# Three rounded passes for key, value and receptance in an RWKV layer, with its token differences and modulation columns reordered

## What is computed

```
    xx = h_shift - h
    xr, xw, xk, xv, xa, xg = [h + xx * mix[j] for j in range(6)]
    r = xr @ wr
    k = xk @ wk
    v = xv @ wv
    ...
        wlog = (w0[d] + jnp.tanh(xw @ w1[d]) @ w2[d]).astype(jnp.float32)
        a = jax.nn.sigmoid((a0[d] + (xa @ a1[d]) @ a2[d]).astype(jnp.float32))
```

## Time and profile before

| | |
|---|---|
| Median of 3 executions | 3708.02 us (3697.62 to 3708.9) |
| The profiled execution | 3712.69 us, its span 3710.8 us |
| Busy: TensorE, VectorE, ScalarE, GpSimd | 3444.4, 1473.4, 1101.6, 315.3 us |
| Granted TensorE clock, mean of the span | 0.973 |
| Chain that ended last, by engine | PE 76%, DVE 9%, DMA 8%, ACT 3%, POOL 2% |
| The RWKV projections lie between | 948 and 1276 us of the span |

### The profile page before, as it was taken

One profiled execution on the slowest core, in us unless ns is written; L12 is line 12 of the kernel. 1 busy time (PEld: TensorE's weight loads), 2 busy tenths in 40 slices (PEclk: granted clock), 3 DMA queues, 4 the chain that ended last, 5 costly groups with the idle time before them and its releaser, 6 DMA issues.

```text
span 3710.8 us, 64299 instructions
## 1 busy us (share of the span) xinstructions
PE 3444.4 (93%) x28700; PEld 2265.9 (61%) x28700; DVE 1473.4 (40%) x2588; ACT 1101.6 (30%) x2075; POOL 315.3 (8%) x260
## 2 busy tenths in 40 slices
PE   6999999999799999999779887899999999999998
PEld 4555344335357588888434332266888876878886
DVE  2232001014542267777531000157753435674343
ACT  4121111113442255554210000144532323543131
POOL 0000000000100234444100000001000001000000
PEclk8989999999799999999989999999999999999999
DMA  9236988985434344431527999930242212133320
GB/s 352 81 158 272 376 333 330 380 341 223 153 118 157 94 97 86 85 72 43 183 113 323 421 413 421 421 115 18 74 148 91 91 51 76 41 116 111 91 91 23
DMA packets 340518, 666.56 MB, mean 180 GB/s; under 512 B 156601, under 2 KB 250297, under 8 KB 284945
## 3 DMA queue, kind: packets, MB, share of 16 engines
q1 hardware_dynamic: 330128, 633.14, 47.5%
q10 hardware_dynamic: 6912, 18.88, 1.3%
q0 software_dynamic: 3200, 10.42, 0.8%
HBM read 630.92 MB, written 31.46 MB: 178 GB/s over the span
## 4 chain that ended last, share of the span: by engine, by line
PE 76%; DVE 9%; DMA 8%; ACT 3%; POOL 2%; issue 1%; SPq 1%; DVEq 0%; ACTq 0%; POOLq 0%
PE ps L1072 14%; PE ps L1077 5%; PE ps L714 4%; DMA ring<-in_moe_wu 4%; PE ps L3202 3%; PE ps L3201 3%; PE ps L3200 3%; PE ps L3218 3%; PE ps L3219 3%; PE ps L3217 3%; PE ps L630 3%; PE ps L631 2%; PE ps L632 2%; PE ps L1507 2%; POOL ring L1896 2%; PE ps L1532 2%
## 5 line engine op out<-in xcount | busy, mean ns | idle before, releaser
L1072 PE MATMUL ps<-ring,H 128*64 128x512 f32 x2016 | 483.8, 602 | 43.4 <-DMA ring<-in_moe_wu 32.9
L1183 DVE TENSOR_TENSOR scr<-ps,scr 128x512 f32<-128x512 f32 x32 | 22.1, 692 | 901.2 <-PE ps L1077 495.6
L1072 PEld LDWEIGHTS ps<-ring,H 128*64 128x64 f32 x2016 | 146.7, 137 | 323.9 <-issue 231.9
L1072 PE MATMUL ps<-ring,scr 128*64 128x512 f32 x1016 | 246.2, 601 | 30.0 <-DMA ring<-in_moe_wd 25.9
L3182 DVE TENSOR_TENSOR ring_rounded<-ring,scr_rounded 128x2048 fp32r<-128x2048 f32 x64 | 146.7, 2293 | 216.6 <-ACT scr_rounded L3175 216.3
L3217 PE MATMUL ps<-scr_rounded,ring_rounded 128*128 128x512 f32 x512 | 201.9, 394 | 1.6 <-DVE ring_rounded L3182 1.6
L3200 PE MATMUL ps<-scr_rounded,ring_rounded 128*128 128x512 f32 x512 | 202.8, 396 | 0.0
L3202 PE MATMUL ps<-scr_rounded 128*128 128x512 f32 x512 | 202.6, 396 | 0.0
L3219 PE MATMUL ps<-scr_rounded 128*128 128x512 f32 x512 | 202.4, 395 | 0.0
L3201 PE MATMUL ps<-H_rounded,scr_rounded 128*128 128x512 f32 x512 | 202.3, 395 | 0.0
L3175 ACT ACTIVATE scr_rounded<-ring 128x2048 fp32r<-128x2048 f32 x64 | 122.2, 1909 | 242.7 <-PE ps L3219 242.7
(11 more groups left out here) (524 smaller groups left out, 6798.2 us busy)
## 6 DMA issues: line engine op xcount, KB each, us to landing
ring<-in_moe_wu SPq DMA_DIRECT2D x128, 1024.0 KB, 8.7
ring<-in_moe_wd SPq DMA_DIRECT2D x127, 1024.0 KB, 9.4
ring<-in_moe_wg SPq DMA_DIRECT2D x124, 1024.0 KB, 9.5
ring<-in_mlp_w SPq DMA_DIRECT2D x64, 1024.0 KB, 5.4
ring<-in_ada_w SPq DMA_DIRECT2D x48, 1024.0 KB, 12.0
ring<-in_w_in SPq DMA_DIRECT2D x14, 1024.0 KB, 5.3
ring<-in_w_out SPq DMA_DIRECT2D x8, 1024.0 KB, 5.4
st_kka<-scr ACTq DMA_DIRECT2D x16, 384.0 KB, 3.5
```

The source lines that it names most:

```text
L1072: ins = pe.matmul(bx[64 * n:64 * n + 64, :], stat_x(k), w[:, k % 4, :], start=k == 0, stop=k == KT - 1)
```

## The change

- Key, value and receptance use `products`: three rounded passes per product. Their weights get a second ring slot each; the mixed activations' high parts (`mixed_high`, ScalarE) lie in three ring slots `xh.0` to `xh.2`, their low parts (`mixed_low`, VectorE) overwrite XJ. Key tiles 0 and 1, the six token tiles of the first value weight, and receptance tiles 0 and 1 are each one batch that goes through the eight k together. VectorE and ScalarE get the splits at fixed places in their orders.
- Token differences of tiles 0 to 3 move to GpSimd, tiles 4 to 7 to VectorE; GpSimd's wait at the end of n1 goes.
- Modulation blocks 44 to 47 are multiplied before the first low-rank product; ScalarE handles them between its tile shifts.
- The a-branch (`down("la", ...)`, its mixes and eviction) moves ahead of the decay products; the key mixes move into the decay loop.

```
 LASTS = {f"i{l}.hh.{n}": f"i{l}.z.1" for l in range(2) for n in range(2)}
 LASTS["yh"] = "i0.ckv"
+LASTS.update({"xh.0": "wr.3.hi", "xh.1": "wr.3.hi", "xh.2": "wv.3.hi", "a2": "wk.3.hi"})
...
-    cols("wk", a["rw_wk"][0])
-    cols("wv", a["rw_wv"][0])
-    cols("wr", a["rw_wr"][0])
+    for n in range(3):
+        plan.append((f"xh.{n}", None))
+    for nm in ("wk", "wv", "wr"):
+        cols(nm, a[f"rw_{nm}"][0], add=split)
...
         def phase(eng, e, name):
 
             marks[f"ph.{name}.{e}"] = (e, count[e])
+            if name == "n1":
+                return
...
         XX = S(0, KT, TA)
-        XJ = S(6144, KT, TA)
+
+        def mix_parts(k, s0, sn):
+
+            if s0 >= TX:
+                o = TC * k + s0 - TX
+                return ring_r[:, place["xh.2"][0], o:o + sn], XJ_r[:, k, s0:s0 + sn]
+            o = TX * (k % 4) + s0
+            return ring_r[:, place[f"xh.{k // 4}"][0], o:o + sn], XJ_r[:, k, s0:s0 + sn]
+
+        def mixed_high(act, j, k):
+
+            if later(act, f"xj{j}.{k}"):
+                act.wait_ge(*at(f"xj{j}.{k}"))
+            for n in range(3) if (j, k) == (2, 0) else ():
+                slot_free(act, f"xh.{n}")
+            for s0, sn in jsegs(j):
+                did(A_, act.activation(mix_parts(k, s0, sn)[0], XJ[:, k, s0:s0 + sn], ACT.Copy).then_inc(scalar_done, 1))
+            marks[f"xjh{j}.{k}"] = (A_, count[A_])
+
+        def mixed_low(dve, j, k):
+
+            if later(dve, f"xjh{j}.{k}"):
+                dve.wait_ge(*at(f"xjh{j}.{k}"))
+            for s0, sn in jsegs(j):
+                hi, lo = mix_parts(k, s0, sn)
+                did(V, dve.tensor_tensor(lo, XJ[:, k, s0:s0 + sn], hi.bitcast(F32), ALU.subtract).then_inc(vector_done, 1))
+            marks[f"xjl{j}.{k}"] = (V, count[V])
...
-            down("lw", "w1", 1, None, between=lambda k: ada_tensor(pe, ADA_N1[0] + 3 + k, ADA_N1[0] + 4 + k == ADA_N1[1]) if ADA_N1[0] + 3 + k < ADA_N1[1] else None)
+            down("lw", "w1", 1, None)
+            down("la", "a1", 4, None)
...
-            down("la", "a1", 4, None)
...
-            for m in range(KT):
-                w = weight(pe, f"wk.{m // 2}")
...
-                        ins = pe.matmul(b[:, 0:sn], w[:, k, (m % 2) * P:(m % 2) * P + P], XJ[:, k, s0:s0 + sn],
-                                        start=k == 0, stop=k == KT - 1)
-                    did(T_, ins.then_inc(tensor_done, 1), f"k.{m}.{s0}")
...
+            def lora_a(m):
...
+            def products(items, j):
+
+                banks = [bank(pe, key)[:, 0:sn] for key, sn, ops in items]
+                for k in range(KT):
+                    if later(pe, f"xjl{j}.{k}"):
+                        pe.wait_ge(*at(f"xjl{j}.{k}"))
+                    for b, (key, sn, ops) in zip(banks, items):
+                        ins = three(pe, b, *ops(k), k == 0, k == KT - 1)
+                        if k == KT - 1:
+                            did(T_, ins.then_inc(tensor_done, 1), key)
+
+            def column(tag, wname, m, s0, sn):
+
+                w = split_weight(pe, f"{wname}.{m // 2}")
+                o = (m % 2) * P
+                return f"{tag}.{m}.{s0}", sn, lambda k: ([x[:, k, o:o + P] for x in w], mix_parts(k, s0, sn))
+
+            products([column("k", "wk", m, s0, sn) for m in range(2) for s0, sn in SEGS], 2)
+            marks["wf.wk.0"] = (T_, count[T_])
+            lora_a(0)
+            head_norm(0)
+            lora_a(1)
+            for m in range(2, KT):
+                products([column("k", "wk", m, 0, TX)], 2)
+                head_norm(m - 1)
+                products([column("k", "wk", m, TX, TC)], 2)
+                if m % 2:
+                    marks[f"wf.wk.{m // 2}"] = (T_, count[T_])
+                if m == KT - 1:
+                    marks["xjfree2"] = (T_, count[T_])
+                lora_a(m)
             head_norm(KT - 1)
             marks["wf.a2"] = (T_, count[T_])
...
+            def token_rows(n, tt):
+
+                w = split_weight(pe, f"wv.{n}")
+                return f"v.{n}.{tt}", 256, lambda k: (mix_parts(k, tt * P, P), [x[:, k, :] for x in w])
             for n in range(4):
-                w = weight(pe, f"wv.{n}")
-                for tt in range(TA // P):
...
-                        ins = pe.matmul(b[:, 0:256], XJ[:, k, tt * P:tt * P + P], w[:, k, :], start=k == 0, stop=k == KT - 1)
...
+                if n == 0:
+                    products([token_rows(0, tt) for tt in range(TA // P)], 3)
+                for tt in range(TA // P) if n else ():
+                    products([token_rows(n, tt)], 3)
                 marks[f"wf.wv.{n}"] = (T_, count[T_])
-            marks["xjfree3"] = (T_, count[T_])
-            linear_tensor(pe, "r", "wr", xj(0), jsegs(0), lambda k: f"xj0.{k}")
-            marks["xjfree0"] = (T_, count[T_])
+            marks["xjfree3"] = marks["wf.xh.2"] = (T_, count[T_])
+            products([column("r", "wr", m, 0, TX) for m in range(2)], 0)
+            marks["wf.wr.0"] = (T_, count[T_])
+            for m in range(2, KT):
+                products([column("r", "wr", m, 0, TX)], 0)
+                if m % 2:
+                    marks[f"wf.wr.{m // 2}"] = (T_, count[T_])
+            marks["xjfree0"] = marks["wf.xh.0"] = marks["wf.xh.1"] = (T_, count[T_])
             first_step = next(units())
             chunk_products(pe, *first_step[0])
             chunk_products(pe, *first_step[1])
...
-        XX_POOL = (5, 6, 7)
+        XX_POOL = (0, 1, 2, 3)
...
-            for k in range(KT):
-                if k not in XX_POOL:
-                    shifted(dve, V, vector_done, k)
+            first_mix(0)
+            first_mix(1)
+            for k in range(4, KT):
+                shifted(dve, V, vector_done, k)
+                first_mix(k - 2)
+            first_mix(KT - 2)
+            first_mix(KT - 1)
+
+            def mix_k(n, k):
+                j = order[n]
+                if later(dve, f"xjfree{order[n - 1]}"):
+                    dve.wait_ge(*at(f"xjfree{order[n - 1]}"))
+                did(V, dve.scalar_tensor_tensor(XJ[:, k, :], XX[:, k, :], col("mix", 8 * j + k), H[:, k, :],
+                                                ALU.mult, ALU.add).then_inc(vector_done, 1), f"xj{j}.{k}")
                 if k:
-                    first_mix(k - 1)
-            first_mix(KT - 1)
+                    mixed_low(dve, j, k - 1)
+                if k == KT - 1:
+                    mixed_low(dve, j, k)
...
                     did(V, dve.scalar_tensor_tensor(to[:, k, 0:w], XX[:, k, 0:w], col("mix", 8 * j + k), H[:, k, 0:w],
                                                     ALU.mult, ALU.add).then_inc(vector_done, 1), f"xj{j}.{k}")
+                    if j in (2, 3, 0) and k:
+                        mixed_low(dve, j, k - 1)
+                if j in (2, 3, 0):
+                    mixed_low(dve, j, KT - 1)
+            mix(1)
             for d in range(2):
                 for m in range(KT):
...
                     did(V, dve.tensor_scalar(ST[s], ST[s], -HALF, None, ALU.mult).then_inc(vector_done, 1), f"lw{d}.{m}")
-                    if d == 0 and m == 0:
-                        mix(1)
-            mix(2)
+                    if d == 0:
+                        mix_k(2, m)
+                    if d == 1 and m == 3:
+                        split_low(dve, "wk.0")
             for m in range(KT):
+                if m in (1, 3, 5):
+                    split_low(dve, f"wk.{m // 2 + 1}")
                 if m == KT - 1:
+                    split_low(dve, "wv.0")
                     mix(3)
...
                 marks[f"kout.{m}"] = (V, count[V])
+            for n in range(1, 4):
+                split_low(dve, f"wv.{n}")
+            split_low(dve, "wr.0")
             mix(4)
+            split_low(dve, "wr.1")
             mix(5)
+            split_low(dve, "wr.2")
...
-            for un in first_step:
+            for n, un in enumerate(first_step):
                 chunk_scan(dve, *un)
+                if n:
+                    split_low(dve, "wr.3")
                 chunk_tildes(dve, *un)
...
             lora("lw", 0, ACT.Tanh, SEGS)
+            lora("la", 1, ACT.Copy, SEGS)
             for d in range(2):
                 for m in range(KT):
...
-            lora("la", 1, ACT.Copy, SEGS)
+                    if 1 <= n <= KT:
+                        mixed_high(act, 2, n - 1)
+                    if d == 1 and m == 2:
+                        split_high(act, "wk.0")
             for m in range(KT):
...
                     for s0, sn in SEGS:
+                        for k in range(4 * d + 2 * (s0 > 0), 4 * d + 2 * (s0 > 0) + 2) if m == KT - 1 else ():
+                            mixed_high(act, 3, k)
                         t = tile(act, f"a{d}.{m}.{s0}")
...
                 marks[f"rn.{m}"] = (A_, count[A_])
+                if m in (0, 2, 4):
+                    split_high(act, f"wk.{m // 2 + 1}")
+                if m == 6:
+                    split_high(act, "wv.0")
```

(12 more changed lines are left out.)

23 lines of the change are left out of this document (5 added, 18 removed).

## The result

The changed kernel takes 3716.0 us (median of 10 runs, 3713.8 to 3719.2) against 3706.9 for the kernel before in the same comparison (3697.6 to 3711.6): ratio 1.0028, 95% interval 1.0019 to 1.0037. The forecast was 4.7 us less; it is 9.1 more. The total lies inside the range, but the sign is wrong: the difference is small, 0.28%, yet the interval leaves out 1 and the two ranges don't touch.

The account below looks back on a forecast made before the run. It took TensorE as bound by the length of its f32 products in key, value and receptance. Front -8.9, key -5.7, value +1.1, receptance +8.8 made 4.7 us less: 3703.3, range 3685 to 3722.

Parts of the forecast that it names:

- The forecast's products (42.8): Key, value and receptance: three rounded passes take 178.5 us on TensorE against 221.3 in f32, 42.8 less.
- Front: Up to the first key product: key starts at 1018.7 against 1027.6, 8.9 us earlier.
- The modulation columns cost nothing: Front: their ScalarE work fits between tile shifts, TensorE having idled; without that cover 4 us.
- Key: Key projection: 98.4 us against 104.1, 5.7 less, of 16.5 that its products save.
- the period of 11.25 us a tile: Key loop: 8.30 of products plus 2.95 for a-products and head norms; ScalarE nearly full at 9.9 plus split work.
- Value: Value projection: 88.9 us against 87.8, 1.1 more, its 14.7 saved being lost in waits.
- Receptance: Receptance projection: 64.9 us against 56.1, 8.8 more, with TensorE waiting 12.9 for the last weight tile's split.
- All later chunk work follows as before: After receptance: the remaining chunk work stays as it was, adding no term to the sum.
- The parts at the low clock: TensorE work at the low clock in the projections: 1.5 us in key, 2 in value, 2 in receptance.
- The clock rival (3): TensorE stays at 1.2 GHz in a-product and decay loop, short waits cost 2 each: 19.4 more, 3722.7; chance 0.20.
- Rival 2: Every wait is hidden; the products' 42.8 arrive with the front's 8.9: 3656 us; chance 0.07.
- the exclusion of VectorE and GpSimd: Front: the two engines lock each other out, so times add to 27.9; without it, 9.0 us better.

Follow-up runs that it names:

- experiment 5: Kernel before with the changed front alone, all three projections staying f32: 3674.8 us, ratio 0.9925.
- Experiments 3: Changed kernel with each key weight split one tile earlier on ScalarE and VectorE: 3712.8 us, ratio 1.0025 to the kernel before.
- experiment 10: Changed kernel with key weights split one tile earlier and the two decayed-key stores issued on GpSimd's queue, not ScalarE's: 3715.8 us, ratio 1.0025.
- 11: Changed kernel, key weights split one tile earlier, GpSimd storing decayed keys once they stand, next tile's first outputs awaiting only these: 3701.1 us, ratio 0.9986.
- Experiment 4: Changed kernel with the second value weight's high part ahead of the last key stores on ScalarE: 3708.4 us, ratio 1.0007 to the kernel before.
- experiment 8: Changed kernel with the key mixes' eight low parts moved to the decay loop's second half: 3713.5 us, ratio 1.0022 to the kernel before.

## Why the prediction was wrong

The forecast's products (42.8) and most of its queue reasoning hold. What failed, by its own steps:

- **Front (8.9 earlier; 18.7 measured).** Mis-sized twice. The last mix came at 24.9 and not 30.0, because I added GpSimd's four tiles (9.0) to the gains in full; they cost VectorE 3.4 on the gains and 1.3 on the first two mixes and the first difference (2.78 for two mixes that take 0.93 each elsewhere, 1.03 for 0.61). Of these 5.1 us, 3.4 reach the end of the a-product. And the decay loop took 29.9 and not 36.3, because the clock held to 988. The two make the 9.8. Its direction was right, and it is the whole gain of the change: experiment 5 shows 28.9 here. The price that the rounded key puts on it, 10.2, I had booked as the old state of the clock, not as a cost.
- **The modulation columns cost nothing.** Nothing in the runs speaks against it: in experiment 5 the front with them forward is shorter, though they were not tried alone.
- **Key (5.7 less; 5.3 more measured).** This is the failed step: the period of 11.25 us a tile. The tiles came 13.8 apart. I took ScalarE as the nearly full engine and never walked the staging tiles round: outputs 5.9, store issues 3.3 and a landing of about 4 make some 13 us a tile. The old period of 13.31 just covered that, and the 8.30 of products plus 2.95 that I put in its place does not. A single 7.4 us wait for the landing of a store stood in the trace of before. The wait that I had before tile 2 (7.0) was a wait of 4.8 for a bank, one product earlier, and 0.3 for the split; those before tiles 4 and 6 (1.5 each) were 4.3 and 2.8. Another 2.9 of the 11.0 is the first batch, 19.5 and not 16.6, since it began at the low clock. Experiments 3, 10 and 11 settle the cycle: with the splits early and two stores at once the period is 11.0 and key takes 92.7.
- **Value (1.1 more; 6.9 measured).** The mechanism was right, the size was off: the batch began at F + 19.1 and not F + 15.1 (F is key's end), since the first value split stood behind the last key outputs (mixes from F + 4.3, not 3.0) and ScalarE's last sigmoids behind all high parts. The second weight's wait was 3.5, just the F + 34 to F + 37.5 of the sum, but the three tiles behind it took 53.2 and not 51.4, at a clock of 0.75 to begin with. Experiment 4 shows that this short wait costs more than its length.
- **Receptance (8.8 more; 14.3 measured).** The mechanism was right in each link: g1 ahead of the streams, scans, exponentials, wr.3. Its sizes were short: streams at R + 35.1 and not 30.4 (R is value's end), the first scan 10.1 behind them and not 8.1. The g1 load came at R + 32.3 and not 28.2: the batch at R began 2.3 late, so the wr.1 output stood at R + 19.4 and not 17.3 (the 4.2 us wait before it was in the forecast), and that output and the next, partly at 0.58, took 12.8 and not 10.9.
- **"All later chunk work follows as before"** holds: the stages differ by 7.9 us and the medians by 9.1.
- **The parts at the low clock** (1.5 in key, 2 in value, 2 in receptance) measured some 19 in the three stages: I had booked some 2 us three times, and there were eight such waits, at some 2 us each, with the key start besides. This is the second failed size.
- **The clock rival (3)** had the right sign and the wrong place: the a-product ran at the full clock, and the price lay behind the waits of the three projections. A rival for a staging or store cycle was not on my list. Rival 2's reason for small odds, the value weight behind the key stores, was real, and worth 7.7.

On the exclusion of VectorE and GpSimd, the forecast cited the Trainium skill ("SBUF — State Buffer", "Who interferes with whom"). By its rule GpSimd's six subtractions during the gains, 7.4 us by their records, would come on top of 8.56: an estimate of 16.0. The gains took 11.93 with GpSimd beside them and 8.56 without: the direction agrees, and the measured price is less than half. If GpSimd's records contain time in which it was itself held up, the price of a full lock would be less than their sum, so the rows don't show whether the lock is partial or the records are long.

## What to carry to other kernels

When one engine's work in a loop shrinks, walk every buffer of that loop round once (written, issued, landed, written again) and hold the sum against the new period; a single wait for a landing in the old trace is the warning. When operands must be split, place each split where its input is ready and ask what stands ahead of it in each in-order queue: 17 us hung on one misplaced split and 15 on two stores. Price a wait of TensorE at its length and some 2 us more, however short it is: several short waits cost more than one long one of the same sum. And run the parts of a bundled change alone: here a front worth 32 us was hidden by projections that cost 41.

## What the hardware showed that I had not expected

- Five stores of 384 KB that leave together land later when they are issued quicker: a `kka` store took a median 5.6 us from issue to landing in experiment 10, 3.5 in the change. Of what was tried, only issuing two of them earlier, beside VectorE's work, shortened the cycle.
- TensorE's clock at equal products: the decay products ran all at 1.00 in 19.7 us when fed without a wait, and fell to 0.50 after waits of 0.78 us each, for 10 us more, and also after waits of 0.21 us each (experiment 8, 27.9 us). The same loop had run at 0.50 in the kernel before too, so this stage's clock depends on what is put beside it.
- A wait of TensorE costs its length and then a stretch of work at the low clock: eight waits of 2.3 to 15.5 us, 51.5 together, lost an estimated 1.7 to 2.8 each behind them, which with the key start is the 19 of the three stages. It isn't certain in every case: behind the same 2.3 us wait the clock was 0.58 in the change and 1.00 in experiment 4.
